# Eleven RMS norms: all eight squares added on VectorE, one addend left for TensorE

## The reference

```python
def rms_norm(x, g):
    xf = x.astype(jnp.float32)
    y = xf * lax.rsqrt(jnp.mean(xf * xf, axis=-1, keepdims=True) + RMS_EPS)
    return (y * g.astype(jnp.float32)).astype(x.dtype)

h = h + rms_norm(m, g[1])
f = sq_relu_mlp(rms_norm(h, g[2]), w_up[layer], w_down[layer])
h = h + rms_norm(f, g[3])
```

## Time and profile before

| | |
|---|---|
| median of 3 runs | 2607.49 us (2606.31 to 2608.08) |
| profiled execution, its time | 2603.99 us |
| its span, first to last instruction | 2602.2 us |
| TensorE busy | 2552.5 us, 98% of the span |
| VectorE busy | 1615.5 us, 62% |
| ScalarE busy | 1022.8 us, 39% |
| GpSimd busy | 1000.8 us, 38% |
| mean granted TensorE clock | 0.996 |

### The profile page before, as it was taken

How to read it: one execution, slowest core, us unless ns; L and a number is a source line. 1 busy time by engine, 2 the same in 40 slices (tenths; PEclk the granted TensorE clock), 3 DMA queues, 4 the chain that set the end, 5 groups by cost and what they waited for, 6 DMA issues and landing times.

```text
span 2602.2 us, 35877 instructions
## 1 busy us (share of the span) xinstructions
PE 2552.5 (98%) x13742; PEld 2205.9 (85%) x13742; DVE 1615.5 (62%) x3050; ACT 1022.8 (39%) x1578; POOL 1000.8 (38%) x547
## 2 busy tenths in 40 slices
PE   8999999999999999999999999999999999999998
PEld 6778899999999988888888788888889767988887
DVE  6754888899999978888888556500215265630213
ACT  5434334444444433333333534522323355442331
POOL 3322453634454523333332143444442313254442
PEclk9999999999999999999999999999999999999999
DMA  4222245779999989999999332333322321233321
GB/s 150 98 87 82 97 138 161 216 268 351 389 393 396 319 310 342 359 351 344 359 348 324 119 98 73 98 97 97 98 97 82 105 78 60 67 114 98 97 97 49
DMA packets 193483, 488.36 MB, mean 188 GB/s; under 512 B 18568, under 2 KB 85016, under 8 KB 193056
## 3 DMA queue, kind: packets, MB, share of 16 engines
q1 hardware_dynamic: 156448, 351.83, 40.5%
q0 software_dynamic: 36864, 134.23, 13.8%
HBM read 442.98 MB, written 42.88 MB: 187 GB/s over the span
## 4 chain that ended last, share of the span: by engine, by line
PE 89%; DVE 5%; DMA 2%; ACT 2%; issue 1%; POOL 0%; SPq 0%; DVEq 0%; ACTq 0%
PE ps L307 28%; PE ps L309 27%; PE ps L308 27%; PE ps L1725 1%; PE ps L495 1%; PE ps L2632 1%; PE ps L2720 1%; DVE tmpb L1116 1%; DVE wl L296 1%; PE ps L1535 1%; DMA rsb<-in_un,idx 1%; DVE hT L2365 0%; PE ps L2684 0%; PE ps L541 0%; DMA lg<-gG_scratch 0%
## 5 line engine op out<-in xcount | busy, mean ns | idle before, releaser
L296 POOL TENSOR_TENSOR wl<-wraw,wh 128x1024 fp32r<-128x1024 f32 x254 | 619.9, 2447 | 988.5 <-ACT wh L288 911.8
L288 ACT ACTIVATE wh<-wraw 128x1024 fp32r<-128x1024 f32 x487 | 513.9, 1059 | 1193.8 <-PE ps L309 1187.3
L307 PE MATMUL ps<-Xh,wh 128*128 128x384 f32 (+2 forms) x2336 | 836.8, 358 | 15.5 <-DVE wl L296 9.1
L309 PE MATMUL ps<-Xh,wl 128*128 128x384 f32 (+2 forms) x2336 | 820.0, 351 | 0.0
L308 PE MATMUL ps<-Xl,wh 128*128 128x384 f32 (+2 forms) x2336 | 819.9, 351 | 0.0
L307 PEld LDWEIGHTS ps<-Xh,wh 128*128 128x128 f32 x2336 | 441.1, 189 | 61.8 <-issue 17.5
L309 PEld LDWEIGHTS ps<-Xh,wl 128*128 128x128 f32 x2336 | 440.9, 189 | 39.2
L308 PEld LDWEIGHTS ps<-Xl,wh 128*128 128x128 f32 x2336 | 441.7, 189 | 36.2
L296 DVE TENSOR_TENSOR wl<-wraw,wh 128x1024 fp32r<-128x1024 f32 x233 | 284.8, 1223 | 83.4 <-ACT wh L288 82.5
L307 PE MATMUL ps<-wh,Hh 128*128 128x512 f32 x768 | 299.2, 390 | 2.6 <-ACT gl L1782 1.6
L309 PE MATMUL ps<-wh,Hl 128*128 128x512 f32 x768 | 298.8, 389 | 0.0
(11 more groups left out here) (317 smaller groups left out, 3044.3 us busy)
## 6 DMA issues: line engine op xcount, KB each, us to landing
wraw<-in_uT SPq DMA_DIRECT2D x128, 512.0 KB
wraw<-in_v SPq DMA_DIRECT2D x128, 512.0 KB
wraw<-in_up SPq DMA_DIRECT2D x128, 512.0 KB
gA_scratch<-gl SPq DMA_DIRECT2D x122, 192.0 KB
gl<-gA_scratch SPq DMA_DIRECT2D x122, 192.0 KB
gG_scratch<-gbuf SPq DMA_DIRECT2D x64, 256.0 KB
lg<-gG_scratch SPq DMA_DIRECT2D x64, 256.0 KB
wraw<-in_w_q SPq DMA_DIRECT2D x24, 512.0 KB
```

What stands on the lines that cost most here:

```text
L288: act.activation(wh[:, n % 4, :], wraw[:, n % 4, :], ACT.Copy).then_inc(s_wh, 1)
L296: pool.tensor_tensor(wl[:, n % 4, :], wraw[:, n % 4, :], wh[:, n % 4, :].bitcast(F32), ALU.subtract).then_inc(s_wl, 1)
L307: pe.matmul(o, ah, bh, start=start, stop=False)
L309: return pe.matmul(o, al, bh, start=False, stop=stop)
```

## The change

All eight squares are added on VectorE in each of the eleven norms, and `root_pe` has `sqacc` as its only addend. Whole norms get one more `sum_add`, for tile 7. Norms in halves get `half_add`, one add of 128 x 256 for tile 6 and one for tile 7 in each half, placed directly ahead of the reciprocal of that half in VectorE's stream. `root_pe` now waits for `s_add` alone. The two small norms "s0" and "s1" of the state-space part use other functions and stay as they are.

```diff
-        i, sq, add, sb, hf = i + 1 + two, sq + n + 2 * two, add + max(0, n - 2 - two), sb + n - 1, hf + 2 * two
+        i, sq, add, sb, hf = i + 1 + two, sq + n + 2 * two, add + (0 if name[0] == "s" else n - 1 + 2 * two), sb + n - 1, hf + 2 * two
...
+    def half_add(dve, name, hf, m=6):
+
+        a, ts = N[name], HALF[hf]
+        k = a.add + 5 + 2 * hf + m - 6
+        dve.wait_ge(s_sq, a.sq + 2 * hf + m + 1)
+        dve.wait_ge(s_add, k)
+        dve.tensor_tensor(sqacc[:, ts], sqacc[:, ts], sqb[:, (a.sb + m - 1) % 2, ts], ALU.add).then_inc(s_add, 1)
...
-        parts = [sqacc, sqb[:, (a.sb + a.n - 2) % 2, :]]
+        parts = [sqacc]
         if hf is None:
-            pe.wait_ge(s_add, a.add + a.n - 2)
-            pe.wait_ge(s_sq, a.sq + a.n)
+            pe.wait_ge(s_add, a.add + a.n - 1)
         else:
-            parts.append(sqb[:, (a.sb + a.n - 3) % 2, :])
-            pe.wait_ge(s_add, a.add + a.n - 3)
-            pe.wait_ge(s_sq, a.sq + a.n + 2 * hf)
+            pe.wait_ge(s_add, a.add + 5 + 2 * hf + 2)
...
-        for c in range(1, 7):
+        for c in range(1, 8):
             sum_add(dve, "in", c)
...
         out_half_dve(dve, 0, 7)
+        half_add(dve, "q", 0)
+        half_add(dve, "q", 0, 7)
         root_dve(dve, "q", 0)
...
             if hf == 0:
+                half_add(dve, "q", 1)
+                half_add(dve, "q", 1, 7)
                 root_dve(dve, "q", 1)
...
-        for c in range(3, 7):
+        for c in range(3, 8):
             sum_add(dve, "fin", c)
...
             if c >= 2:
                 sum_add(dve, "av", c - 1)
+        sum_add(dve, "av", 7)
...
-        for c in range(1, 7):
+        for c in range(1, 8):
             sum_add(dve, "up0", c)
...
-        return {1: lambda: split_lo(dve, tile0 + 2), 4: lambda: split_lo(dve, tile0 + 3),
-                5: lambda: root_dve(dve, name, 1)}
+        def second_root():
+            half_add(dve, name, 1)
+            half_add(dve, name, 1, 7)
+            root_dve(dve, name, 1)
+
+        return {1: lambda: split_lo(dve, tile0 + 2), 4: lambda: split_lo(dve, tile0 + 3), 5: second_root}
...
             def second_root_k():
+                half_add(dve, sq_, 1)
+                half_add(dve, sq_, 1, 7)
                 root_dve(dve, sq_, 1)
                 split_lo(dve, W_K + 3)
...
             def second_7():
                 last(1, 7)
+                half_add(dve, sq_, 1)
+                half_add(dve, sq_, 1, 7)
                 root_dve(dve, sq_, 1)
```

More of the change, by code:

```diff
@@ L2329, in gmlp_dve @@
             sum_add(dve, "mo", m)
+        half_add(dve, "mo", 0)
+        half_add(dve, "mo", 0, 7)
         root_dve(dve, "mo", 0)
         add_norm_dve(dve, "mo", uT, 8, "up0", "g2", 16, norm_beside(dve, "mo", F0), s_mo)
-        for c in range(1, 7):
+        for c in range(1, 8):
             sum_add(dve, "up0", c)
@@ L2538, in ffn_dve @@
         last(0, 7)
+        half_add(dve, sq_, 0)
+        half_add(dve, sq_, 0, 7)
         root_dve(dve, sq_, 0)
@@ L2859, in att_dve @@
             sum_add(dve, "o2", m)
+        half_add(dve, "o2", 0)
+        half_add(dve, "o2", 0, 7)
         root_dve(dve, "o2", 0)
         add_norm_dve(dve, "o2", kTs, 40, "up1", "g2", 48, norm_beside(dve, "o2", F1), s_oe)
-        for c in range(1, 7):
+        for c in range(1, 8):
             sum_add(dve, "up1", c)
```

## The result

The kernel became slower: 2624.0 us in the median of six executions (2622.0 to 2628.0) against 2606.9 us for the kernel before on the same chip, a ratio of 1.0068 with an interval of 1.0055 to 1.0081. That is 17 us, where 11.6 were forecast. The profiled execution is the slowest of the six, 2628.04 us with a span of 2626.3, so its marks show more than the medians do.

A forecast was written before the change was run, and what follows sets the result against it. TensorE, busy 98% of the span, was taken to bound the kernel. Issuing 14.2 us less but waiting 22 us more gave +8.0, the clock +3.6: 2607.5 + 11.6 = 2619 us, range 2610 to 2624.

The forecast's parts named there:

- What goes and what comes: 128 matmuls of line 495 go, 14.2 us; six adds of 128 x 512 and twenty of 128 x 256 come.
- The five first roots: First halves of mo, o2, f0, f1, q: little or no wait, changes of -0.88, -0.88, -0.75, -0.76, -0.52 us.
- The second roots: Second halves of q, mo, f0, o2: TensorE waits for VectorE's late adds, costing +1.40, +3.23, +3.84, +3.2 us.
- the replay: Trace stretches around each root with starts kept, moving only what new waits move; +8.0 us in all, without the clock.
- "up0", "k", "up1": Three whole norms: the seventh add waits for GpSimd's subtraction, root 1.76 us late, +0.87 us per norm.
- "av": forecast 0: Root of av: TensorE waits 0.92 us for the square root anyway, fewer matmuls only lengthen this; change 0.
- The clock: Half clock behind the waits of f0, mo, o2: 0 to 1.7 us each, taken as 1.2, together +3.6 us.
- the clock falls after 'q' and the three shorter waits too, or stays low longer: Rival at TensorE's new waits, including q, up0, k, up1: more loss than forecast, 2624 to 2628 us; chance 13%.
- VectorE first in "up0", "k", "up1": Rival: at these norms VectorE's seventh add goes ahead of GpSimd, 5.3 us less, 2614 us; chance 10%.
- Absorbed later: Rival: later waits of TensorE for other engines swallow the delays, time stays at about 2607 us; chance 11%.
- Adds hidden: Rival: TensorE reaches the second roots after VectorE's adds and keeps all or some of its gain, 2593 us; chance 6%.

The follow-up runs named there:

- kernel with the wait alone: Kernel before; TensorE waits at second roots of q, mo, f0, o2 for VectorE's one-column copy; repeated so that no tile moves: 2627.6 us, ratio 1.0079.
- the one without these four roots: Changed kernel with the old three addends back in the second roots of q, mo, f0 and o2: 2606.1 us, ratio 1.0000.
- the waits filled: Changed kernel, with TensorE issuing matmuls that nobody reads during its waits at the second roots of q, mo, f0, o2: 2616.5 us, ratio 1.0050.
- the kernel with the second roots alone: Kernel before, with the two adds and single addend only in the second roots of q, mo, f0 and o2: 2625.6 us, ratio 1.0077.

## Why the forecast was right or wrong

**What goes and what comes: right.** 128 matmuls less at 0.111 us, adds of 0.42 and 0.95 us a pair. Left alone the adds cost nothing clear of the noise (2607.2 us), and the full saving shows where nothing waits: -0.89 and -0.90 at "in" and "fin". The five first roots saved less than forecast, -3.04 for -3.79: -0.44 at "q", -0.71 at "mo" and "o2", -0.59 at "f0" and "f1". The add of tile 7 ends 0.46 us behind its square, as taken, but TensorE starts 0.15 us after the add's end and not 0.05, so that "mo" and "o2" wait too. TensorE comes 0.15 to 0.50 us after the last square in the trace before, where the forecast writes 0.3 to 0.8.

**The second roots: right in place and length.** The four waits were forecast within 0.3 us. That the wait carries the loss, and neither the adds nor the lost matmuls, is shown by the kernel with the wait alone (+22 us) and by the one without these four roots (no difference from before). With the waits filled, the four steps agree with the replay to 0.05 us.

**"up0", "k", "up1": right.** The engines do take turns: the roots came 1.87 us late, for 1.76, and net +3.05 for +2.61. That it is GpSimd's second subtraction which holds the add up is shown by putting it behind. The Trainium skill (SBUF — State Buffer, section "SBUF: two separate sides") says that whichever of the two starts first holds the ports for its whole instruction; the trace agrees (5.27 us for two adds beside GpSimd's 5.19). GpSimd, which had been waiting, went between two adds 0.1 us apart at all three norms. What I did not have was that a wait of 1.7 us can be followed by the half clock too, which in this trace it was at none of the three.

**"av": forecast 0.** Its wait for the square root did grow, from 0.92 to 1.83 us, as argued: the saved matmuls only lengthened it, and without the clock nothing was gained or lost. The wait in the timeline of PE:

```profile
1493.54 0.80 PE L307 MATMUL ps<-wh,Xh 128*128 128x512 f32 x1 [1.83 <-ACT rst L533]
```

The +1.3 is a stretch at 0.50 on the work behind it:

```profile
1493.00:1496.30 3.30, 2.76 (x7) 2.19 (x8) 1.99 (x3) 2.70 (x5) 3.30 (x3) 0.50 0.52 159
```

It is not the change's: such a stretch fell there in 4 of 10 executions with the old wait, and in 2 of 4 with the new one.

**The clock: the term that failed.** The step reads: "I bound the price of each by 0 and 1.7 and take 1.2", for three waits, 3.6 us in all. Measured were 11.3 us at four roots (2.6 to 3.0 each) in the profiled executions, of which the medians show about 5. By the trace it is this term that takes the time out of the range. The kernel with the waits filled leaves a second, smaller one: its medians lose 12 us where the replay without a clock gives 8.0. Some 2 us of that are the short stretches at 0.50 behind "up0", "k" and "up1" (an estimate: 6 of 15 waits, 1.6 us each, three waits), which the forecast put at nothing. Three things in the clock term were wrong. The length: the only stretch behind a pause that I had read lasted 3.3 us, and I took this for the upper bound; behind waits of 3.7 to 5.0 us it was 6.8 us in eleven of twelve cases, and 10.2 in one. And I let part of it fall into the wait: in the changed kernel the low clock was granted from about the end of the wait on, and lay on dense work. (In the kernel with the second roots alone 2.1 to 3.3 us of it did fall into three of the waits.) The count was wrong too: "q", with 2.1 us, I had held safe because a pause of 2.4 us had left the clock alone; here 3 of 4 lost it. One row each way was no bound, and the trace before has another row that I passed over. At its very end TensorE waits 1.58 us, and from 1.0 us behind that wait the clock is at 0.50, so that the twelve matmuls there take 1.82 us and not 12 x 0.111 = 1.33:

```profile
2589.59 0.35 PE L495 MATMUL ps<-ones,sqdg 128*128 128x1 f32 x2 [1.58 <-ACT sqb L465]
...
2590.60:2594.00 3.40, 2.03 (x9) 1.64 (x8) 0.91 (x3) 0.26 (x1) 0.00 (x0) 0.50 0.01 2
```

The Trainium skill (TensorE: Matmul & The Clock Gate, section "HAM oscillation — how this bites in real kernels") prices such a wait by half of the throttled time. With 6.8 us that is 3.4, an estimate by that rule; 2.6 to 3.0 were measured.

With this term as the trace has it the forecast's own +8.0 for matmuls and waits becomes +19, and the medians show +17 (14 to 21). Of the 24 us between the two profiled executions, another 1.2 are the smaller savings and the larger cost of "up0", "k" and "up1", and the rest is scatter of the kind seen at "av" and in the mixer. The rival that came true is the last, "the clock falls after 'q' and the three shorter waits too, or stays low longer", which had 13%. It does stay low longer and falls at "q"; behind the three shorter waits it falls in other kernels' executions (6 of 15), and not in the changed kernel's.

**The other rivals.** VectorE first in "up0", "k", "up1": fell (5.27 us for two adds). Absorbed later: fell, the marks behind each spread keep their shift to the next norm within 0.3 us, except where a stretch at 0.50 falls in between. Adds hidden: fell, and moving them up shows what it asks for; even then only "q" and "f0" gained.

**Open.** What decides whether a wait of 1 to 2 us is followed by the half clock, since the same kernel does it in one place and not in another of the same code. And why stretches at 0.50 come now and then where TensorE had not waited anew, as behind the second roots of "mo" and "o2", each in two kernels that leave it as before, and once for 10.2 us at "fin" in the second kernel with the wait alone. And why the medians give back only half of what the clock costs in the traces. The runs settle none of these.

## What to carry to other kernels

Before work is moved from a full engine to one with slack, find where in its own stream the other engine is when the result is wanted: here eight matmuls, together 0.9 us, were traded for waits of 2 to 5 us. The same adds three chunks earlier at two roots, left out at the two where none of the places tried gained, and GpSimd held back behind the last of them, turned 17 us of loss into 10 us of gain. And a wait of TensorE in a dense kernel is not priced by its length alone: behind those of 2.1 to 5.0 us here another 2.6 to 3.0 us each were lost to the clock.

## What the hardware showed that was not expected

- Stretches of 6.8 us at 0.50 behind waits of 3.7 to 5.0 us, and of 3.4 us behind some waits of 1.7 us. Matmuls that nobody reads, issued in the wait, kept the clock at 1.00 in all four places and took 11.3 us off these stretches in the trace and about 5 us off the median, with no other change.
- A tile of 4 bytes per partition, allocated ahead of the large operands `Hh`, `Hl`, `Fh` and `Fl`, raised the pitch of the 128 x 512 matmuls that read them from 0.227 to 0.233 or 0.234 us, 20 to 24 us in the kernel. `Fh` and `Fl` are the moving operand there, `Hh` and `Hl` the stationary one; matmuls on unmoved tiles kept their pitch. Which places in memory are slow was not tried.
- At "up0", "k" and "up1" GpSimd's waiting subtraction went ahead of VectorE's next add, which was ready 0.1 us after the last. A semaphore wait that holds GpSimd back for 1.4 us at "up0", and its like at the other two, saved 7.7 us in the medians.
